# The first half of a state-space input product taken by pairs of token parts, between the parts of its norm

## The chip, the cores and the metric

One core of a Trainium2 chip runs the whole program. The time is the device time of one execution, in microseconds (us); it was 1764.43 us as the median of three runs.

## What is computed

Two transformer-like blocks over 512 tokens of 1024 channels, all in fp32. The change lies at the seam of the two: the layer norm at the end of the first block, then the root-mean-square norm and the input product of the second block's state-space mixer.

```python
x = _layernorm(DEEPNORM_ALPHA * x + ffn, ln2_g[l], ln2_b[l])      # end of the first block
...
h = rms_norm(x, mix_norm[layer])                                   # second block, layer 0
u = (h @ w_in).reshape(bsz, seq, SSM_GROUPS, SSM_GROUP)            # 64 groups of 16 channels
# then a scan along the tokens in each group, computed by chunks of T = 8 tokens (64 chunks)
```

## The kernel before

**Numbers.** Each fp32 operand of a large product is split into a high and a low part, and a product takes three matmuls (high-high, high-low, low-high). Activations lie turned, as `a_hi` and `a_lo` [channel in partition, 8 channel blocks, 512 tokens]. Weights pass through a ring of six slots in chunks of 512 KB: SP (SyncE) loads a chunk into `w_raw` when the slot's last chunk has been used (L1141), ScalarE (ACT) scales it by the norm's gain (L1190, two instructions, for these chunks alone) and makes the high part (L1195), GpSimd (POOL) makes the low part (L1045). The low part lies where the raw chunk lay, so a slot is free only when TensorE has used both. How far ACT makes chunks ahead is set by `make(count)`, held back by `limit`; a step that reads a PSUM bank first makes LEAD = 4 chunks ahead of that bank's.

**The seam.** The last down product of the first block's feed-forward runs tile by tile (four tiles of 128 tokens; `rows_by_tile`). Vector engine (DVE) work for a tile `t`: add the product to `x_rows` (L1693, which frees the bank), statistics (L1707, L1713), two passes of the layer norm (L1721, L1723). ACT then squares and sums the row (L1225), takes the root (L1226), and writes the normed row to `xh` (L1392, two buffers), with the root of the next tile's variance (L1369) between. TensorE turns each tile of `xh` by eight transposes into two banks (`mix0[0](t)`, L465), ACT copies them as high part into `a_hi` (L1204) and DVE makes the low part into `a_lo` (L1629). The token order in `a_hi` is changed on the way (`tile_split_s5`): column s*64 + c holds token s of chunk c, so that a matmul over 128 columns gives two token places of all 64 chunks.

**The product.** `w_in` is taken in two column halves. The first half ran as `rows_product`: four banks, one for each 128 columns; for each of four weight chunks all four banks get their 6 matmuls, so that a chunk is done with after 24 matmuls. The second half runs as `rows_by_tile` with the rounds of the state-space recurrence between its parts (`beside_rows`): the eight transposes of `s5_states` need all rows of the first half in `u_c` (they wait for bank ("u", 0, 3) to be freed). The rows go there by `even_rows` on DVE (L2117) and `odd_rows` on ACT (L1411), 64 partitions each.

In between lie other jobs. TensorE works on the recurrence's tables in batches of four groups (`prepare`); ACT evicts the last one, batch 15, in `s5_batch_out` (L1262, L1266), DVE finishes it in L2005, and SP stores it. After the last chunk of the first half ACT issues six loads of stored tables ("records" 0 and 1, L954, L959), SP issues records 2 and 3 behind the load of c7.

The chunks of the first half are called c0 to c3 here, those of the second c4 to c7.

## Time and profile before

| | |
|---|---|
| median of three runs | 1764.43 us (1764.03 to 1764.68) |
| the profiled execution, its own time | 1764.41 us |
| its span | 1762.4 us |
| mean granted TensorE clock | 0.991 of full |
| busy: TensorE matmul, DVE, ACT, GpSimd | 98%, 45%, 38%, 35% |
| idle before the third and fourth turn of the norm | 3.60 and 2.77 us |
| first and last matmul start of the first half product | 599.17, 623.47 us |

The times of the profile are counted from the start of the span; the 2 us between span and time lie around it. An engine's idle time is put down in brackets before an instruction with the work that released it. "PEclk" is the granted TensorE clock as a share of full speed (1.00 is 2.4 GHz, 0.50 is 1.2 GHz).

### The profile page before, as it was taken

The page shows a single profiled execution, that of the slowest core. Times are in us where ns is not written, and L with a number is a line of the kernel's source. Part 1 is how long each engine was busy: PE and PEld are TensorE (multiplying, and loading weights), DVE is VectorE, ACT ScalarE, POOL GpSimd, SP SyncE. Part 2 cuts the span into 40 slices and gives each one's busy share as a digit, 9 for nine tenths or more (in the row PEclk, how much of TensorE's full clock was granted, in tenths as well). Part 3 has the DMA queues.
Part 4 walks back from the last instruction along what each step waited for, and adds up shares of the span by engine and source line. Part 5 has one row for each costly group of instructions (what it writes and reads, how often), then busy time and mean ns, then how long its engine had stood idle before and what let it go on. Part 6 is the DMA issues. An engine that isn't in the chain of part 4 may idle for free.

```text
span 1762.4 us, 22364 instructions
## 1 busy us (share of the span) xinstructions
PE 1721.4 (98%) x8814; PEld 1417.5 (80%) x8814; DVE 793.2 (45%) x1454; ACT 676.2 (38%) x1184; POOL 624.0 (35%) x299
## 2 busy tenths in 40 slices
PE   8999999999999898999999999999899999999999
PEld 6887888887787687789888888888766888888887
DVE  3876899586766547333111111138774411111111
ACT  3333244243243756433222212276764332122221
POOL 5423203304204322424453534434711245345342
PEclk9999999999999899999999999999999999999999
DMA  9422245444445457223333233222201243332322
GB/s 244 96 74 83 72 125 155 148 133 131 140 125 172 142 194 245 80 67 114 97 95 96 93 100 102 84 76 70 73 1 37 72 115 98 94 99 86 107 90 78
DMA packets 241287, 189.58 MB, mean 108 GB/s; under 512 B 40481, under 2 KB 198305, under 8 KB 241185
## 3 DMA queue, kind: packets, MB, share of 16 engines
q1 hardware_dynamic: 239312, 182.79, 34.9%
q10 hardware_dynamic: 1872, 5.37, 0.9%
q8 instruction: 71, 1.16, 0.3%
q14 instruction: 32, 0.25, 0.0%
HBM read 168.73 MB, written 19.40 MB: 107 GB/s over the span
## 4 chain that ended last, share of the span: by engine, by line
PE 88%; DVE 6%; ACT 3%; issue 1%; DMA 1%; POOL 1%; DVEq 0%; SPq 0%; ACTq 0%
PE ps L383 14%; PE ps L385 14%; PE ps L384 14%; PE ps L409 10%; PE ps L411 10%; PE ps L410 10%; PE ps L440 3%; PE ps L442 3%; PE ps L441 3%; PE ps L867 1%; PE ps L897 1%; DVE x_rows L1723 1%; PE ps L859 1%; PE ps L877 1%; ACT w_hi L1195 1%
## 5 line engine op out<-in xcount | busy, mean ns | idle before, releaser
L1045 POOL TENSOR_TENSOR w_lo<-w_raw,w_hi 128x1024 fp32r<-128x1024 f32 (+4 forms) x251 | 587.4, 2350 | 1077.6 <-ACT w_hi L1195 1077.4
L383 PE MATMUL ps<-a_hi,w_hi 128*128 128x512 f32 (+1 forms) x1184 | 442.1, 373 | 0.0
L384 PE MATMUL ps<-a_lo,w_hi 128*128 128x512 f32 (+1 forms) x1184 | 440.4, 372 | 0.0
L385 PE MATMUL ps<-a_hi,w_lo 128*128 128x512 f32 (+1 forms) x1184 | 440.4, 372 | 0.0
L1195 ACT ACTIVATE w_hi<-w_raw 128x1024 fp32r<-128x1024 f32 (+3 forms) x283 | 283.1, 1019 | 207.9 <-DMA w_raw<-in_ffn_w_gate_up_dram 70.7
L383 PEld LDWEIGHTS ps<-a_hi,w_hi 128*128 128x128 f32 x1184 | 223.0, 188 | 40.1 <-issue 1.9
L385 PEld LDWEIGHTS ps<-a_hi,w_lo 128*128 128x128 f32 x1184 | 223.0, 188 | 38.8
L384 PEld LDWEIGHTS ps<-a_lo,w_hi 128*128 128x128 f32 x1184 | 223.1, 188 | 38.3
L2200 DVE TENSOR_TENSOR ev<-ps,xh 128x512 f32<-128x512 f32 x44 | 30.4, 692 | 411.9 <-PE ps L385 382.9
L409 PE MATMUL ps<-w_hi,h_hi 128*128 128x512 f32 x444 | 176.6, 398 | 2.7 <-DVE x_rows L1693 2.7
L411 PE MATMUL ps<-w_hi,h_lo 128*128 128x512 f32 x444 | 175.9, 396 | 0.0
L410 PE MATMUL ps<-w_lo,h_hi 128*128 128x512 f32 x444 | 175.7, 396 | 0.0
L1693 DVE TENSOR_TENSOR x_rows<-ps,x_rows 128x512 f32<-128x512 f32 x72 | 49.2, 690 | 219.5 <-PE ps L411 189.2
L1211 ACT ACTIVATE h_hi<-ev 128x512 fp32r<-128x512 f32 x66 | 41.8, 633 | 235.0 <-DVE ev L2200 195.5
L409 PE MATMUL ps<-w_hi,a_hi 128*128 128x512 f32 (+1 forms) x320 | 126.1, 394 | 1.8 <-DVE a_lo L1629 1.8
L410 PE MATMUL ps<-w_lo,a_hi 128*128 128x512 f32 (+1 forms) x320 | 124.7, 390 | 0.0
L411 PE MATMUL ps<-w_hi,a_lo 128*128 128x512 f32 (+1 forms) x320 | 124.5, 389 | 0.0
L409 PEld LDWEIGHTS ps<-w_hi,h_hi 128*128 128x128 f32 x444 | 84.0, 189 | 23.7 <-issue 4.4
L411 PEld LDWEIGHTS ps<-w_hi,h_lo 128*128 128x128 f32 x444 | 83.9, 189 | 19.8
L410 PEld LDWEIGHTS ps<-w_lo,h_hi 128*128 128x128 f32 x444 | 84.1, 189 | 19.5
L440 PE MATMUL ps<-w_hi,a_hi 128*128 128x512 f32 (+2 forms) x240 | 89.9, 375 | 5.5 <-POOL w_lo L1045 2.2
L1297 ACT ACTIVATE xh<-ps 128x512 f32<-128x512 f32 x44 | 26.3, 598 | 166.4 <-PE ps L385 166.4
(346 smaller groups left out, 2314.6 us busy)
## 6 DMA issues: line engine op xcount, KB each, us to landing
w_raw<-in_ffn_w_gate_up_dram SPq DMA_DIRECT2D x88, 512.0 KB, 3.8
w_raw<-in_w_up_dram SPq DMA_DIRECT2D x44, 512.0 KB, 4.0
w_raw<-in_ffn_w_down_dram SPq DMA_DIRECT2D x40, 512.0 KB, 3.8
w_raw<-in_w_in_dram SPq DMA_DIRECT2D x20, 512.0 KB, 4.3
w_raw<-in_w_down_dram SPq DMA_DIRECT2D x20, 512.0 KB, 3.9
s_records<-stage SPq DMA_DIRECT2D x16, 544.0 KB, 5.3
w_raw<-in_ssm_w_glu_dram SPq DMA_DIRECT2D x16, 512.0 KB, 3.9
rec<-s_records SPq DMA_DIRECT2D x14, 544.0 KB, 5.1
```

The source lines that it names most:

```text
L383: pe.matmul(bank, wh, xh_, start=first, stop=False)
L384: pe.matmul(bank, wh, xl_, start=False, stop=False)
L385: return pe.matmul(bank, wl, xh_, start=False, stop=last)
L409: pe.matmul(o, ah[:, k + kk, s], wh[:, kk, :], start=(n == 0 and kk == 0), stop=False)
L410: pe.matmul(o, ah[:, k + kk, s], wl[:, kk, :], start=False, stop=False)
L411: m = pe.matmul(o, al[:, k + kk, s], wh[:, kk, :], start=False, stop=end)
L440: pe.matmul(o, ah[:, k + kk, s], wh[:, kk, :], start=(k + kk == 0), stop=False)
L441: pe.matmul(o, ah[:, k + kk, s], wl[:, kk, :], start=False, stop=False)
L442: m = pe.matmul(o, al[:, k + kk, s], wh[:, kk, :], start=False, stop=end)
L1045: pool.tensor_tensor(w_lo[:, n % RING, 0:w], w_raw[:, n % RING, 0:w], w_hi[:, n % RING, 0:w].bitcast(F), ALU.subtract).then_inc(lo_made, 1)
L1195: act.activation(w_hi[:, n % RING, 0:w], w_raw[:, n % RING, 0:w], ACT.Copy).then_inc(hi_made, 1)
L1693: ins = v.tensor_tensor(o, b, o, ALU.add)
```

## The change

The first half no longer waits for all four turned tiles. A new token order puts the first 256 tokens at the even columns and the last 256 at the odd ones: column s*64 + 2c + q holds token s of chunk 32q + c. `rows_by_pair` multiplies the even columns (pair q = 0: two banks, four weight chunks, 48 matmuls) and then the odd ones (q = 1) with the same four chunks, which stay in the ring until the second pair has used them. Its first wait is for tiles 0 and 1. The turn of tile 2 stands behind its second chunk, that of tile 3 behind its fourth.

ACT and DVE follow. ACT makes c0 and c1 before batch 15's eviction, splits tiles 0 and 1 together, and makes c2 and c3 between the rows of tile 2 and the splits of tile 2. DVE splits tiles 0 and 1 together before it adds tile 3. A bank of the first half now holds four token places of 32 chunks, so `even_rows` and `odd_rows` take two instructions of 32 partitions each for each bank (four more on either engine). In the second half the rows come out with the two token halves interleaved; `s5_turned` puts them in order for batches 8 to 15 while it copies. The counts of chunks, of matmuls and of bytes are as before.

```diff
--- before.py
+++ after.py
@@ -418,6 +418,34 @@
                     if between:
                         between(n + 1)
 
+            def pair_columns(a, k, q, i):
+                return a[:, k, :].rearrange("p (c q) -> p q c", q=2)[:, q, i * P:i * P + P]
+
+            def rows_by_pair(stage, w, ah, al, nk, c0, cn, per, wait_q, gain, after):
+
+                parts = []
+                for q in range(2):
+                    banks = [open_bank((*stage, 2 * q + i)) for i in range(2)]
+                    pe.wait_ge(lo_ready, wait_q(q))
+                    for n, k in enumerate(range(0, nk, per)):
+                        if q == 0:
+                            parts.append(take_chunk(rows_of(w, k, per, c0, cn), per, cn, gains[:, gain, k:k + per]))
+                        wh, wl = parts[n]
+                        for i in range(2):
+                            o = banks[i][:, 0:cn]
+                            for kk in range(per):
+                                end = k + kk == nk - 1
+                                xh_, xl_ = (pair_columns(a, k + kk, q, i) for a in (ah, al))
+                                pe.matmul(o, xh_, wh[:, kk, :], start=(k + kk == 0), stop=False)
+                                pe.matmul(o, xh_, wl[:, kk, :], start=False, stop=False)
+                                m = pe.matmul(o, xl_, wh[:, kk, :], start=False, stop=end)
+                            if end:
+                                over = close_bank((*stage, 2 * q + i), m)
+                        if q and not end:
+                            chunk_over(m)
+                        after(q, n)
+                chunk_done.append(over)
+
             def rows_by_tile(stage, w, ah, al, nk, c0, cn, per, row0=0, wait_t=None, after=None, gain=None, late=False):
 
                 banks = [None if late else open_bank((*stage, t)) for t in range(TT)]
@@ -701,11 +729,14 @@
 
             ffn("f1", w_up[0], w_down[0], (FF, 0), ln1_turner, prepare, mix0_first)
 
-            for t in range(1, TT):
-                mix0[0](t)
-            mixed = n_split[0]
-            rows_product(("u", 0), ssm_w_in_2[0], a_hi, a_lo, KT, 0, HALF, 2, gain=2,
-                         wait_k=lambda k: mixed - (k < KT // 2))
+            def later_turns(q, n):
+                if (q, n) in ((0, 1), (0, 3)):
+                    mix0[0](2 + n // 2)
+
+            mix0[0](1)
+            chunks_at["u"] = len(chunk_done)
+            rows_by_pair(("u", 0), ssm_w_in_2[0], a_hi, a_lo, KT, 0, HALF, 2, lambda q: mix0[1](2 * q + 1), 2,
+                         later_turns)
             held = []
 
             def s5_bank(name, open_=open_bank):
@@ -967,9 +998,16 @@
 
         def tile_split_s5(k0, t):
 
-            c = slice(t * P // T, (t + 1) * P // T)
-            dst = [a[:, k0:k0 + 4, :].rearrange("p k (s c) -> p k s c", s=T)[:, :, :, c] for a in (a_hi, a_lo)]
+            c = slice((t % 2) * P // T, (t % 2 + 1) * P // T)
+            dst = [a[:, k0:k0 + 4, :].rearrange("p k (s c q) -> p k s c q", q=2, s=T)[:, :, :, c, t // 2]
+                   for a in (a_hi, a_lo)]
             return dst
+
+        def step_rows(bank, j, i):
+
+            q, r = j // 2, slice(NC // 2 * i, NC // 2 * i + NC // 2)
+            return (u_c[NC // 2 * q:NC // 2 * q + NC // 2, 0:32, 4 * (j % 2) + i, :],
+                    bank[r, :].rearrange("c (g k) -> c g k", k=GK))
 
         def ev_s5(e):
             return e.rearrange("p (k c s) -> p k s c", k=4, s=T)
@@ -1304,7 +1342,8 @@
                         for half in range(2):
                             if (g, half) in down_batch:
                                 if down_batch[g, half] == NB:
-                                    limit[0] = chunks_at[("u", 0, 0)] - 3
+                                    limit[0] = chunks_at["u"] + 2
+                                    make(limit[0])
                                 s5_batch_out(down_batch[g, half] - 1)
                             if (g, half) == (2, 0):
                                 load_second_norm()
@@ -1381,22 +1420,35 @@
 
 
             whole = lambda t: (ln_ready, t + 1)
-            ln_deviation(down, 1, 0)
-            limit[0] += 1
-            make(limit[0])
-            for t in range(TT):
-                deviation("mix0", down, whole, t)
-                if t + 1 < TT:
-                    ln_deviation(down, 1, t + 1)
+            def mix0_rows(t):
                 act.wait_ge(rms_made, t + 1)
                 act.activation(xh[:, t % 2, :], x_rows[:, t, :], ACT.Copy, scale=st[:, 8 + t:9 + t])\
                    .then_inc(xh_ready, 1)
-                if t and t < TT - 1:
-                    split_tile("mix0", t - 1, to_a_s5)
-            split_tile("mix0", TT - 2, to_a_s5)
-            split_tile("mix0", TT - 1, to_a_s5)
+
+            def next_chunk():
+                limit[0] += 1
+                make(limit[0])
+
+            ln_deviation(down, 1, 0)
+            deviation("mix0", down, whole, 0)
+            ln_deviation(down, 1, 1)
+            mix0_rows(0)
+            deviation("mix0", down, whole, 1)
+            ln_deviation(down, 1, 2)
+            mix0_rows(1)
+            split_tile("mix0", 0, to_a_s5)
+            split_tile("mix0", 1, to_a_s5)
+            deviation("mix0", down, whole, 2)
+            ln_deviation(down, 1, 3)
+            mix0_rows(2)
+            next_chunk()
+            next_chunk()
+            split_tile("mix0", 2, to_a_s5)
+            deviation("mix0", down, whole, 3)
+            mix0_rows(3)
+            split_tile("mix0", 3, to_a_s5)
             limit[0] = 10 ** 6
-            make(chunks_at[("u", 0, 0)] + 1)
+            make(chunks_at["u"] + 5)
             for i in range(2):
                 act.wait_ge(st_out[i], 16 * (NB // 2))
                 act.wait_ge(k_out[i], 16 * (NB // 2) * T)
@@ -1407,7 +1459,12 @@
                 load_out_part(act, b_)
             def odd_rows(half, j):
                 b = at(("u", half, j))
-                act.wait_ge(u_even, 4 * half + j + 1)
+                if not half:
+                    act.wait_ge(u_even, 2 * j + 2)
+                    step(act.activation(*step_rows(b, j, 1), ACT.Copy))
+                    release(("u", half, j), act.activation(*step_rows(b, j, 3), ACT.Copy))
+                    return
+                act.wait_ge(u_even, 2 * TT + j + 1)
                 release(("u", half, j), act.activation(u_c[:, 32 * half:32 * half + 32, 2 * j + 1, :],
                                                        b[NC:P, :].rearrange("c (g k) -> c g k", k=GK), ACT.Copy))
 
@@ -1417,7 +1474,11 @@
             def s5_turned(b_):
                 if b_ >= RECS:
                     act.wait_ge(*closed(("y", b_ - RECS)))
-                release(("ut", b_), act.activation(u_t[:, b_ % RECS, :], at(("ut", b_))[:, 0:GB * NC], ACT.Copy))
+                o, b = u_t[:, b_ % RECS, :], at(("ut", b_))[:, 0:GB * NC]
+                if b_ >= NB // 2:
+                    o = o.rearrange("p (g q c) -> p g q c", g=GB, q=2)
+                    b = b.rearrange("p (g c q) -> p g q c", g=GB, q=2)
+                release(("ut", b_), act.activation(o, b, ACT.Copy))
 
             def s5_gelu(b_):
                 y = at(("y", b_))[:, 0:2 * P].rearrange("c (g t k) -> c t g k", g=GB, t=T // 2)
@@ -2102,18 +2163,23 @@
             rms(1)
             ln_rows(2, 1, ln_ready)
             split_tile("mix0", 0, to_a_s5)
+            split_tile("mix0", 1, to_a_s5)
             add(3)
             ln_stats(3)
             rms(2)
             ln_rows(3, 1, ln_ready)
-            split_tile("mix0", 1, to_a_s5)
+            split_tile("mix0", 2, to_a_s5)
             rms(3)
-            split_tile("mix0", 2, to_a_s5)
             split_tile("mix0", 3, to_a_s5)
             go(v.memset(zc[:, :, :, 0:1], 0.0))
             go(v.memset(zs[:, :, 0:1], 0.0))
             settle()
             def even_rows(half, j):
+                if not half:
+                    b = full(v, ("u", half, j))
+                    v.tensor_copy(*step_rows(b, j, 0)).then_inc(u_even, 1)
+                    v.tensor_copy(*step_rows(b, j, 2)).then_inc(u_even, 1)
+                    return
                 v.tensor_copy(u_c[:, 32 * half:32 * half + 32, 2 * j, :],
                               full(v, ("u", half, j))[0:NC, :].rearrange("c (g k) -> c g k", k=GK))\
                  .then_inc(u_even, 1)
```

TensorE, behind the turn of tile 1 (`xh` to `ps`; 128x512 are product matmuls). Before, and then with the change:

```order
L465 MATMUL ps<-ident,xh 128x128 [waits bank_free0,xh_ready]
L465 MATMUL ps<-ident,xh 128x128 x3
L465 MATMUL ps<-ident,xh 128x128 [waits bank_free1]
L465 MATMUL ps<-ident,xh 128x128 x3
L465 MATMUL ps<-ident,xh 128x128 [waits bank_free2,xh_ready]
L465 MATMUL ps<-ident,xh 128x128 x3
L465 MATMUL ps<-ident,xh 128x128 [waits bank_free3]
L465 MATMUL ps<-ident,xh 128x128 x3
L465 MATMUL ps<-ident,xh 128x128 [waits bank_free4,xh_ready]
L465 MATMUL ps<-ident,xh 128x128 x3
L409 MATMUL ps<-w_hi,a_hi 128x512 [waits hi_made,lo_ready,lo_made]
L410 MATMUL ps<-w_lo,a_hi 128x512
```

```order
L493 MATMUL ps<-ident,xh 128x128 [waits bank_free0,xh_ready]
L493 MATMUL ps<-ident,xh 128x128 x3
L493 MATMUL ps<-ident,xh 128x128 [waits bank_free1]
L493 MATMUL ps<-ident,xh 128x128 x3
L439 MATMUL ps<-w_hi,a_hi 128x512 [waits hi_made,lo_ready,lo_made,bank_free3,bank_free2]
L440 MATMUL ps<-w_lo,a_hi 128x512
L441 MATMUL ps<-w_hi,a_lo 128x512
L439 MATMUL ps<-w_hi,a_hi 128x512
```

The turns of tiles 2 and 3 are gone from this place, and the first product matmul waits for two weight semaphores, the splits of two tiles, and banks 2 and 3; 24 matmuls later the turn of tile 2 follows.

ACT, at the end of the last down product (w_raw<-w_raw,gains and w_hi<-w_raw are chunk making; k_s<-ps is batch 15's eviction; st<-st the root of tile 0's variance). Before, and then with the change:

```order
L1195 ACTIVATE w_hi<-w_raw 128x512 [waits w_landed5]
L1262 ACTIVATE k_s<-ps 16x112 [waits bank_full5,k_out1,tables_ready]
L1262 ACTIVATE k_s<-ps 16x112 x3
L1266 ACTIVATE stage_99<-ps 128x512 [waits bank_full4,st_out1]
L1369 ACT_TABLE_LOAD
L1369 ACTIVATE st<-st,eps_c 128x1 [waits var_ready]
L1190 ACTIVATE w_raw<-w_raw,gains 128x512 [waits w_landed0]
L1190 ACTIVATE w_raw<-w_raw,gains 128x512
L1195 ACTIVATE w_hi<-w_raw 128x1024 [waits act_step]
```

```order
L1233 ACTIVATE w_hi<-w_raw 128x512 [waits w_landed5]
L1228 ACTIVATE w_raw<-w_raw,gains 128x512 [waits w_landed0]
L1228 ACTIVATE w_raw<-w_raw,gains 128x512
L1233 ACTIVATE w_hi<-w_raw 128x1024 [waits act_step]
L1228 ACTIVATE w_raw<-w_raw,gains 128x512 [waits w_landed1]
L1228 ACTIVATE w_raw<-w_raw,gains 128x512
L1233 ACTIVATE w_hi<-w_raw 128x1024 [waits act_step]
L1300 ACTIVATE k_s<-ps 16x112 [waits bank_full5,k_out1,tables_ready]
L1300 ACTIVATE k_s<-ps 16x112 x3
L1304 ACTIVATE stage_99<-ps 128x512 [waits bank_full4,st_out1]
L1408 ACT_TABLE_LOAD
```

One chunk stood behind the first root; two stand ahead of the batch's eviction now.

ACT, behind the record loads (u_c<-ps are the odd rows of the first half). Before, and then with the change:

```order
L959 DMA rec_109<-s_records 128x1088
L1190 ACTIVATE w_raw<-w_raw,gains 128x512 [waits w_landed4]
L1190 ACTIVATE w_raw<-w_raw,gains 128x512
L1195 ACTIVATE w_hi<-w_raw 128x1024 [waits act_step]
L1190 ACTIVATE w_raw<-w_raw,gains 128x512 [waits w_landed5]
L1190 ACTIVATE w_raw<-w_raw,gains 128x512
L1195 ACTIVATE w_hi<-w_raw 128x1024 [waits act_step]
L1190 ACTIVATE w_raw<-w_raw,gains 128x512 [waits w_landed0]
L1190 ACTIVATE w_raw<-w_raw,gains 128x512
L1195 ACTIVATE w_hi<-w_raw 128x1024 [waits act_step]
L1411 ACTIVATE u_c<-ps 64x32x16 [waits u_even,bank_full6]
L1411 ACTIVATE u_c<-ps 64x32x16 [waits u_even,bank_full7]
```

```order
L990 DMA rec_109<-s_records 128x1088
L1464 ACTIVATE u_c<-ps 32x32x16 [waits u_even,bank_full2]
L1465 ACTIVATE u_c<-ps 32x32x16 [waits act_step]
L1464 ACTIVATE u_c<-ps 32x32x16 [waits u_even,bank_full3]
L1465 ACTIVATE u_c<-ps 32x32x16 [waits act_step]
L1228 ACTIVATE w_raw<-w_raw,gains 128x512 [waits w_landed5]
L1228 ACTIVATE w_raw<-w_raw,gains 128x512
L1233 ACTIVATE w_hi<-w_raw 128x1024 [waits act_step]
L1228 ACTIVATE w_raw<-w_raw,gains 128x512 [waits w_landed0]
L1228 ACTIVATE w_raw<-w_raw,gains 128x512
L1233 ACTIVATE w_hi<-w_raw 128x1024 [waits act_step]
L1464 ACTIVATE u_c<-ps 32x32x16 [waits u_even,bank_full0]
```

Three chunks (c4, c5 and c6; the records stood behind c3) came ahead of the four odd-row copies. Now the records stand behind c4, and the copies of two banks ahead of c5, those of the other two behind c6.

## Rows read from the trace of the kernel before

**Rows 1.** The page, section 1: busy us, share, instructions.

```profile
PE 1721.4 (98%) x8814; PEld 1417.5 (80%) x8814; DVE 793.2 (45%) x1454; ACT 676.2 (38%) x1184; POOL 624.0 (35%) x299
```

**Rows 2.** Timeline of PE: start us, us, engine, line, operation [idle before <-releaser].

```profile
581.35 1.04 PE L465 MATMUL ps<-ident,xh 128*128 128x128 f32 x8
...
591.74 1.97 PE L465 MATMUL ps<-ident,xh 128*128 128x128 f32 x8 [3.60 <-ACT xh L1392]
596.49 1.97 PE L465 MATMUL ps<-ident,xh 128*128 128x128 f32 x8 [2.77 <-ACT xh L1392]
599.17 0.77 PE L409 MATMUL ps<-w_hi,a_hi 128*128 128x512 f32 x1 [0.72 <-DVE a_lo L1629]
...
606.02 0.39 PE L409 MATMUL ps<-w_hi,a_hi 128*128 128x512 f32 x1
...
623.70 0.39 PE L440 MATMUL ps<-w_hi,a_hi 128*128 128x512 f32 x1
```

**Rows 3.** Windows: length, busy of PE, PEld, DVE, ACT, POOL, PEclk, DMA, GB/s.

```profile
592.00:599.00 7.00, 3.68 (x16) 2.88 (x15) 4.83 (x8) 5.33 (x11) 0.00 (x0) 0.50 0.51 155
```

**Rows 4.** Timeline of PE at the chunk c7.

```profile
630.17 0.47 PE L440 MATMUL ps<-w_hi,a_hi 128*128 128x512 f32 x1 [0.19 <-POOL w_lo L1045]
```

**Rows 5.** Timeline of ACT at batch 15 and at the first norm rows.

```profile
571.01 1.05 ACT L1262 ACTIVATE k_s<-ps 16x112 f32<-16x112 f32 x4 [10.39 <-PE ps L664]
...
579.77 1.14 ACT L1392 ACTIVATE xh<-x_rows,st 128x1024 f32<-128x1024 f32 x1
```

**Rows 6.** SP's issue of c1, and its time from issue to landing.

```profile
565.92 0.37 SPq L1141 DMA_DIRECT2D w_raw<-in_ssm_w_in_dram  x1
...
w_raw<-in_ssm_w_in_dram SPq DMA_DIRECT2D x1, 512.0 KB, 5.3
```

**Rows 7.** Timeline of ACT during the half product.

```profile
600.34 1.06 ACT L1195 ACTIVATE w_hi<-w_raw 128x1024 fp32r<-128x1024 f32 x1
...
605.12 0.82 ACTq L954 DMA_DIRECT2D rec<-s_records  x2
...
607.93 1.34 ACT L1190 ACTIVATE w_raw<-w_raw,gains 128x512 f32<-128x512 f32 x2 [1.90 <-issue]
...
616.34 1.34 ACT L1190 ACTIVATE w_raw<-w_raw,gains 128x512 f32<-128x512 f32 x2 [3.67 <-DMA w_raw<-in_ssm_w_in_dram]
```

**Rows 8.** Timeline of DVE in the norm.

```profile
573.08 0.69 DVE L1693 TENSOR_TENSOR x_rows<-ps,x_rows 128x512 f32<-128x512 f32 x1
...
587.47 1.28 DVE L1629 TENSOR_TENSOR a_lo<-ps,a_hi 128x512 fp32r<-128x512 f32 x2
588.67 0.68 DVE L1693 TENSOR_TENSOR x_rows<-ps,x_rows 128x512 f32<-128x512 f32 x1
...
590.11 0.21 DVE L1713 BATCH_NORM_AGGREGATE st<-st 128x2 f32<-128x12 f32 x1
```

**Rows 9.** Timeline of POOL (GpSimd), three low parts.

```profile
601.47 7.09 POOL L1045 TENSOR_TENSOR w_lo<-w_raw,w_hi 128x1024 fp32r<-128x1024 f32 x3 [21.24 <-ACT w_hi L1195]
```

**Rows 10.** Timeline of PE at 1167, and the windows view around it.

```profile
1167.48 0.37 PE L440 MATMUL ps<-w_hi,a_hi 128*128 128x288 f32 x1 [1.99 <-POOL w_lo L1045]
...
1166.00:1174.00 8.00, 6.52 (x39) 6.55 (x40) 1.68 (x3) 3.77 (x7) 3.16 (x2) 0.79 0.01 2
```

**Rows 11.** SP's issue of c6, and its time from issue to landing.

```profile
607.57 0.37 SPq L1141 DMA_DIRECT2D w_raw<-in_ssm_w_in_dram  x1
...
w_raw<-in_ssm_w_in_dram SPq DMA_DIRECT2D x1, 512.0 KB, 8.8
```

**Rows 12.** Line L1411: durations min/median/max in ns, first and last start.

```profile
L1411 ACT ACTIVATE u_c<-ps x8: 593/596/597, 620.7 to 659.1; 64x512 f32<-64x512 f32 x8
```

**Rows 13.** Line L1204 from 640 and in the norm; page, section 5.

```profile
L1204 ACT ACTIVATE a_hi<-ps x8: 1097/1116/1216, 655.5 to 721.2; 128x512 fp32r<-128x512 f32 x8
...
L1204 ACT ACTIVATE a_hi<-ps x8: 572/584/597, 585.6 to 598.5; 128x512 fp32r<-128x512 f32 x8
...
L383 PEld LDWEIGHTS ps<-a_hi,w_hi 128*128 128x128 f32 x1184 | 223.0, 188 | 40.1 <-issue 1.9
```

## The prediction

> **What bounds the kernel now.** First the busy shares: TensorE is busy for 98% of the span [rows 1], so what the change can win is idle or slowly clocked TensorE time, and the question is where it is. TensorE's timeline at the change answers: three idle places lie side by side [rows 2]. The third turn of the norm waits 3.60 us for its rows, the fourth 2.77 us, and the first product of the state-space input waits 0.72 us more. The granted clock of that stretch is 0.50, the 1.2 GHz level [rows 3]; the matmuls run at that level until 604.4. From 599.17 to 606.02 lie 18 matmul starts in 6.85 us; the 78 starts from 606.02 to 623.70 take 17.68 us, 0.227 us each [rows 2], so the slow clock costs about 2.8 us of the product.
>
> I call the weight chunks of the two halves c0 to c3 and c4 to c7, and the matmul stream's arrival at c7 (630.17 before, where it waited 0.19 us for that chunk's low part [rows 4]) the end of the stage: behind it the code has the same work and TensorE is the bound again, so the gain or loss there is the gain or loss of the kernel.
>
> **Ideal saving.** The second turn is over at 588.1 (591.74 - 3.60). With two turns of 0.8 us (as 581.35 to 582.14 [rows 2]) and 96 matmuls of 0.227 us behind it and no wait, the half product would be over at 611.5 instead of 623.7. So at most 12.2 us are there. Both ACT and VectorE (DVE) get in the way, step by step:
>
> **1. Two chunks ahead of the last table batch.** ACT now makes c0 and c1 before it evicts the kernel block of batch 15, which it did at 571.01 [rows 5]. c1 is issued at 565.92 and lands 5.3 us later, at 571.2 [rows 6]. Making a chunk takes ACT 1.34 + 1.06 = 2.4 us [rows 7]. The eviction starts at 573.6, 2.6 us late. DVE's add of tile 0 began right behind it, at 573.08 [rows 8], and DVE then works without a real pause through the four tiles; so the whole norm shifts by 2.6 us. The first rows xh would be ready at 579.77 + 1.14 + 2.6 = 583.5 [rows 5], where TensorE wants them at 581.35 [rows 2]: 2.2 us of new idle, and the second turn ends at 590.3.
>
> **2. Start of the first pair.** DVE reaches its first splits at 587.47 + 2.6 = 590.1 and now makes four instead of two (1.28 us a pair [rows 8]): 592.7. The two banks of the pair are those of the down product's third and fourth tile, and the add of the fourth tile stands behind the four splits: 0.7 us more [rows 8]. So the pair starts at 593.4, after 3.1 us of idle. 24 matmuls at full clock take it to 598.9, the third turn to 599.7.
>
> **3. c2 and c3.** The statistics of tile 3 come 1.65 us after the start of its add (588.67 to 590.32 before [rows 8]), at 594.3; ACT then takes a root of 0.3 us and the rows of 1.14 us: 595.8. Then it makes c2 and c3, to 598.2 and 600.5. GpSimd adds 2.36 us for each low part (7.09 us for three [rows 9]): 600.5 and 602.9. TensorE at full clock would wait 0.8 us here. After the idle of 3.1 us I expect a stretch at 1.2 GHz: an idle of 1.99 us at 1167 was followed by one, and over the 8 us around it the mean granted clock was 0.79, so that 8 x 0.21 = 1.7 us of clock were lost [rows 10]. Of 1.7 us, 0.8 is hidden by this wait and 0.9 counts. Turn three ends at 601.4, c2 and c3 are used until 606.9, the fourth turn ends at 607.7.
>
> **4. Second pair.** It waits for the splits of tile 3: one ACT split 0.6 and one DVE split 0.7 behind the turn, 1.4 us with the gaps (0.72 before, where the slow turn hid the rest). 609.1, and 48 matmuls later 620.0. That is 3.7 us before the old 623.70.
>
> **5. The second half gives it back.** c0 and c1 are kept until the second pair has used them, so c6 can only be loaded into c0's slot at 609.1 + 2.7 = 611.8. ACT ends its last split at 608.4, makes c4 until 610.7 and begins to issue the state records 0.9 us before that, at 609.8. That is the distance of before: 605.12 against the end of c3 at 600.34 + 2 x 2.3 + 1.06 = 606.0 [rows 7]. So records and c6 still meet: 2.1 us after the first record, 2.45 before. I take the landing time of before, 8.8 us [rows 11]: c6 lands at 620.7. ACT finishes the record issues at 612.6 (2.8 us, to the 607.93 of before [rows 7]), makes four odd-row copies of tiles 0 and 1, and c5, until 617.5, and then waits for c6, until 623.1 with its making. Only then come the four odd-row copies of tiles 2 and 3, which have to be over before TensorE may turn the first states. A copy of 64 partitions takes 0.596 us [rows 12]. No row shows one of 32 partitions: between half and the same, I take the same, since the elements in a partition are the same: 2.5 us for four, 625.6. TensorE arrives at 622.7 and idles 2.9 us. ACT makes c7 from 625.6 to 628.0, and GpSimd its low part to 630.4. TensorE had c7 at 630.17 before, and now at 630.5.
>
> **Sum.** Idle and clock removed -3.7 us at the end of the half product, wait for the odd rows and c7 +4.0 (10.5 us from there to c7 against 6.5): +0.3. The profiled execution has 1764.41 us beside a span of 1762.4 and a median of 1764.43, so both bases agree; the forecast is **1764.7 us**.
>
> DVE's even-row copies double as well, at no cost: the four of tiles 0 and 1 fall into the second pair, and the four of tiles 2 and 3, 0.7 us each from 618.6 on, are over at 621.4, before ACT is ready for them at 623.1. Without that cover they would bound ACT; rival B counts that. SP issues the same transfers in the same order, with later slots. Batch 15's stores stand between c3 and c4; c4 is wanted at 608.4 by ACT, long after.
>
> **The step of 8 bytes.** The new column order makes ACT and DVE write the split rows, and TensorE load its stationary tiles, at every second fp32. No such row exists. The nearest is a split written with a step of 64 bytes: ACT 1.116 us against 0.584 for the one with contiguous runs [rows 13]. So the bounds are nothing and +0.53 us per split, and for a load of 0.188 us [rows 13] nothing and double. I take nothing and keep the other end for a rival. The Trainium skill's page "SBUF — State Buffer", section "Door 1: The DMA port swizzle", says that SBUF works in lines of 16 bytes and that two accesses to a line are enough for full bandwidth; two fp32 at 8 bytes fall into one line. By that rule the term is zero, and the 64-byte row agrees with it.
>
> **Rivals.** *A, slower:* the 8-byte step costs like the 64-byte one. Four DVE splits before the first pair give about +1.6, the last tile +0.9, in sum 1764.7 + 2.5 = 1767.2 for the writers alone. If the loads double as well, the matmul distance goes from 0.227 to 0.376 us: 96 x 0.15 = 14.3, less some 1.5 of waits: about 1780. It turns slower once a load costs over 0.227 us, the cover that the running matmul gives. For it: a 1.9-fold row. Against it: the 8 times larger step. *B, faster:* c6 does not meet the records and lands after 5.3 us, as c1 did. Then ACT has c6 by 619.9, the odd rows follow the closing of the banks (620.0, plus two copies on each engine) to 622.6, no state waits, and c7's low part is there at 627.4: -2.8, so 1761.6; without the slow stretch 0.9 less, 1760.7. For it: some of the records may be through when c6 is issued, if the first pair ends later than the records' issue assumes. Against it: both follow the same pair, and their distance (2.1 against 2.45 us) hardly changes. *C, the clock:* the idle of 1.4 us before the second pair is also followed by a slow stretch: +1.7 in the pair, about +1.3 at the end: 1766.0. For it: 0.72 us of idle among slow turns left the clock at 0.50 before. Against it: the pair ahead is full of matmuls.
>
> **Chances.** Forecast 0.51, C 0.10, B 0.29, A 0.10. A measurement can tell about 0.2%, 3.5 us. Forecast and C (0.61) lie within; of B about 0.22 lies beyond (it needs the full clock or an early norm as well), 0.07 within; of A 0.06 beyond; errors of several steps in one direction take 0.09 from what lies within and add 0.01 to faster and 0.08 to slower. Faster 0.23, same 0.63, slower 0.14. The range takes most of B and the mild part of A: 1760.0 to 1768.0; what it leaves out is about 0.17.
>
> **What would show it.** ACT's eviction of batch 15 near 573.6, and xh of tile 0 at 583.5. The first pair beginning near 593.4 behind DVE's add of tile 3. The half product ending near 620. A wait of some 3 us of the first states' turn for ACT's odd rows, ACT waiting for c6 before them. c7 reached near 630.5. Stationary loads at 188 ns and splits at 0.59 us. The forecast is wrong if c6 lands within 6 us of its issue, if ACT isn't held by c1's landing, or if the loads at the 8-byte step are longer.

## The result and the profile after

| | before | after |
|---|---|---|
| median of 20 runs, us | 1764.0 (1761.58 to 1765.0) | 1766.55 (1763.94 to 1768.69) |
| ratio to before | | 1.0017, 95% interval 1.0011 to 1.0023 |
| profiled execution, us, and its span | 1764.41, 1762.4 | 1763.94, 1761.9 |
| c7 reached | 630.17 [rows 4] | 629.58 |
| end of the half product | 623.70 [rows 2] | 619.57 |
| from c7 to the end of the span | 1132.2 | 1132.3 |

The change costs 2.6 us by the medians (0.14%; 0.17% by the ratio), just inside the 0.2% that I called no change; the interval reaches a little beyond. The profiled execution is the fastest of the 20 runs of the change, so its profile shows the stage, and it doesn't by itself show why the median is 2.6 us above it.

The page, section 1, answers [rows 1]: TensorE (PE) is busy 2 us less, with the same instructions.

```profile
PE 1719.4 (98%) x8814; PEld 1415.1 (80%) x8814; DVE 795.8 (45%) x1458; ACT 679.0 (39%) x1188; POOL 624.0 (35%) x299
```

Timeline of TensorE in the profile after, against [rows 2, 4]: two idle places of 3.60 and 2.77 us are gone, and there are new ones at the first turn (1.55), ahead of the first pair (2.84), at its third chunk c2 (0.46), ahead of the second pair (1.74) and of the first states' turn (2.16).

```profile
583.00 1.09 PE L493 MATMUL ps<-ident,xh 128*128 128x128 f32 x8 [1.55 <-ACT xh L1425]
...
592.69 0.48 PE L439 MATMUL ps<-w_hi,a_hi 128*128 128x512 f32 x1 [2.84 <-DVE x_rows L1754]
...
598.36 1.03 PE L493 MATMUL ps<-ident,xh 128*128 128x128 f32 x8
599.85 0.48 PE L439 MATMUL ps<-w_hi,a_hi 128*128 128x512 f32 x1 [0.46 <-POOL w_lo L1083]
...
605.52 1.04 PE L493 MATMUL ps<-ident,xh 128*128 128x128 f32 x8
608.30 0.48 PE L439 MATMUL ps<-w_hi,a_hi 128*128 128x512 f32 x1 [1.74 <-DVE a_lo L1690]
...
619.57 0.39 PE L468 MATMUL ps<-w_hi,a_hi 128*128 128x512 f32 x1
...
624.62 0.46 PE L756 MATMUL ps<-ident,u_c 64*128 64x64 f32 x4 [2.16 <-ACT u_c L1465]
625.00 0.67 PE L468 MATMUL ps<-w_hi,a_hi 128*128 128x512 f32 x1
...
629.58 0.47 PE L468 MATMUL ps<-w_hi,a_hi 128*128 128x512 f32 x1
```

The windows view of the same profile (length, busy of PE, PEld, DVE, ACT, POOL, PEclk, DMA, GB/s), against [rows 3]: the first pair runs at full clock here. The 0.83 of the second window is the stretch at the 1.2 GHz level that follows the states' idle: at 625.00 above a matmul takes 0.67 instead of 0.39 us.

```profile
592.00:599.00 7.00, 6.31 (x30) 5.34 (x31) 4.25 (x7) 5.34 (x8) 1.68 (x1) 1.00 0.66 203
620.00:630.00 10.00, 7.81 (x35) 5.68 (x34) 1.57 (x4) 7.58 (x12) 5.26 (x5) 0.83 0.80 317
630.00:638.00 8.00, 8.00 (x42) 6.47 (x41) 5.26 (x12) 3.48 (x8) 0.81 (x2) 1.00 0.21 68
```

ACT, against [rows 5, 7]: the eviction of batch 15 starts at 573.05 instead of 571.01, since c1 is only there at 570.60. The records are issued from 608.66, c6 is waited for until 619.66, the four odd-row copies of 32 partitions follow, then c7.

```profile
570.60 1.34 ACT L1228 ACTIVATE w_raw<-w_raw,gains 128x512 f32<-128x512 f32 x2 [1.26 <-DMA w_raw<-in_ssm_w_in_dram]
...
573.05 1.06 ACT L1300 ACTIVATE k_s<-ps 16x112 f32<-16x112 f32 x4
...
608.66 0.82 ACTq L985 DMA_DIRECT2D rec<-s_records  x2
...
619.66 1.34 ACT L1228 ACTIVATE w_raw<-w_raw,gains 128x512 f32<-128x512 f32 x2 [3.38 <-DMA w_raw<-in_ssm_w_in_dram]
...
622.12 0.59 ACT L1464 ACTIVATE u_c<-ps 32x512 f32<-32x512 f32 x1
```

DVE, against [rows 8]: the add of tile 0 (L1754) is 2.05 us late, and the add of tile 3 stands behind four low parts at 591.91.

```profile
575.13 0.69 DVE L1754 TENSOR_TENSOR x_rows<-ps,x_rows 128x512 f32<-128x512 f32 x1
...
589.51 2.48 DVE L1690 TENSOR_TENSOR a_lo<-ps,a_hi 128x512 fp32r<-128x512 f32 x4
591.91 0.68 DVE L1754 TENSOR_TENSOR x_rows<-ps,x_rows 128x512 f32<-128x512 f32 x1
```

SP's issue of c6 and its time from issue to landing, against [rows 11]:

```profile
611.36 0.37 SPq L1179 DMA_DIRECT2D w_raw<-in_ssm_w_in_dram  x1
...
w_raw<-in_ssm_w_in_dram SPq DMA_DIRECT2D x1, 512.0 KB, 8.3
```

The rows at the step of 8 bytes, against [rows 13]: durations of line L1242 (min/median/max in ns), the lines view of PE's weight loads with the mean in ns, and two rows of TensorE's timeline in the second pair. A split takes 0.610 us against 0.584, a load 193 ns against 188. From 610.00 to 615.60 lie 24 matmul starts, 0.233 us each, where the half product before had 0.227 at full clock [rows 2]: over the 96 matmuls that is 0.6 us.

```profile
L1242 ACT ACTIVATE a_hi<-ps x8: 592/610/648, 587.7 to 606.7; 128x512 fp32r<-128x512 f32 x8
...
L439 PEld LDWEIGHTS ps<-w_hi,a_hi 128*128 128x128 f32 x31 | 6.0, 193 | 6.8 <-issue 3.0 <-DVE a_lo L1690 1.9 <-ACT w_hi L1233 0.7
...
610.00 0.39 PE L440 MATMUL ps<-w_lo,a_hi 128*128 128x512 f32 x1
...
615.60 0.39 PE L440 MATMUL ps<-w_lo,a_hi 128*128 128x512 f32 x1
```

The second half, which loads contiguous columns, stands 0.227 us apart with loads of 188 ns in the same profile (from 619.57 on). That the longer load makes the longer distance is not shown, though: the down product before it stands 0.232 us apart with loads of 188 ns.

### The profile page after: what moved, and what is told of

It reads as the page before. It is cut to its first block, busy times and chain, and to the rows that moved or that the text cites. A ratio compares the mean times of both kernels' runs of the same rounds, so it can differ in the third digit from the quotient of the medians.

```text
span 1761.9 us, 22372 instructions
## 1 busy us (share of the span) xinstructions
PE 1719.4 (98%) x8814; PEld 1415.1 (80%) x8814; DVE 795.8 (45%) x1458; ACT 679.0 (39%) x1188; POOL 624.0 (35%) x299
## 4 chain that ended last, share of the span: by engine, by line
PE 87%; DVE 6%; ACT 3%; DMA 2%; issue 2%; POOL 1%; DVEq 0%; SPq 0%; ACTq 0%
PE ps L383 14%; PE ps L384 14%; PE ps L385 14%; PE ps L409 10%; PE ps L411 9%; PE ps L410 9%; PE ps L468 3%; PE ps L470 3%; PE ps L469 3%; PE ps L898 1%; PE ps L928 1%; DMA w_raw<-in_ssm_w_in_dram 1%; PE ps L890 1%; PE ps L908 1%; DVE x_rows L1784 1%
## 5 line engine op out<-in xcount | busy, mean ns | idle before, releaser
L1754 DVE TENSOR_TENSOR x_rows<-ps,x_rows 128x512 f32<-128x512 f32 x72 | 49.2, 690 | 219.5 <-PE ps L411 189.3
L409 PE MATMUL ps<-w_hi,a_hi 128*128 128x512 f32 (+1 forms) x288 | 112.3, 390 | 1.1 <-DVE a_lo L1690 1.1
L410 PE MATMUL ps<-w_lo,a_hi 128*128 128x512 f32 (+1 forms) x288 | 111.1, 386 | 0.0
L411 PE MATMUL ps<-w_hi,a_lo 128*128 128x512 f32 (+1 forms) x288 | 111.1, 386 | 0.0
```

Of the source, the lines that this page charges most:

```text
L409: pe.matmul(o, ah[:, k + kk, s], wh[:, kk, :], start=(n == 0 and kk == 0), stop=False)
L410: pe.matmul(o, ah[:, k + kk, s], wl[:, kk, :], start=False, stop=False)
L411: m = pe.matmul(o, al[:, k + kk, s], wh[:, kk, :], start=False, stop=end)
L1754: ins = v.tensor_tensor(o, b, o, ALU.add)
```

## The experiments

Each kernel was timed beside the kernel before on its chip; where no interval stands, the medians are compared. Unless said otherwise they compute all of the result.

### c1 later, records earlier, both

e1 gives ACT only c0 ahead of batch 15, c1 behind the root of tile 0:

```diff
-                                    limit[0] = chunks_at["u"] + 2
+                                    limit[0] = chunks_at["u"] + 1
...
             ln_deviation(down, 1, 0)
+            next_chunk()
             deviation("mix0", down, whole, 0)
```

> The change, but ACT makes only c0 ahead of batch 15's eviction and c1 behind the root of tile 0's variance. Theory 1 (the whole norm is shifted by c1's landing): the eviction falls back from 573.05 to about 571.0, DVE's add of tile 0 from 575.13 to 573.1, the idle of 1.55 us before the first turn goes, the first pair starts near 590.6 instead of 592.69, and c7 is reached 2 us earlier, near 627.6; the median falls by 2 to 3 us against the change. Rival (ACT's time in the norm is what counts, wherever c1 stands): the first pair starts where it did, and the time stays within 0.7 us of the change.

Measured: 1764.23 us (before on this chip 1763.71), ratio 1.0001, interval 0.9992 to 1.0010. TensorE's timeline in its profile: no wait at the first turn, the steps behind it 1.2 to 2.3 us earlier than in the change (590.44 for 592.69, 623.41 for 624.62), but the states' turn still waits 2.34 us, and c7 comes at 628.38, 1.2 us earlier and not 2. Here the first pair has the slow stretch that the profile of the change hasn't.

```profile
581.14 1.04 PE L493 MATMUL ps<-ident,xh 128*128 128x128 f32 x8
...
590.44 0.48 PE L439 MATMUL ps<-w_hi,a_hi 128*128 128x512 f32 x1 [2.50 <-DVE x_rows L1755]
...
623.41 0.46 PE L756 MATMUL ps<-ident,u_c 64*128 64x64 f32 x4 [2.34 <-ACT u_c L1466]
```

e2 moves the issues of records 0 and 1 on ACT from behind c4 to ahead of the last tile's splits:

```diff
             mix0_rows(3)
-            split_tile("mix0", 3, to_a_s5)
-            limit[0] = 10 ** 6
-            make(chunks_at["u"] + 5)
             for i in range(2):
...
                 load_out_part(act, b_)
+            split_tile("mix0", 3, to_a_s5)
+            limit[0] = 10 ** 6
+            make(chunks_at["u"] + 5)
```

> The change, but ACT issues the records behind the rows of tile 3 (near 603.3, where it idled 2.84 us) instead of behind c4. Theory 2 (c6 is late because it shares the DMA queues with the records, and the odd rows stand behind it): c6 lands within 6 us of its issue at 611.1 instead of 8.6, the wait of 2.16 us before the first states' turn falls below 0.5, c7 is reached near 626.5 instead of 629.58; the median falls by about 3 us. Rival (c6 is late because its slot is free so late): c6 still lands near 619, c7 moves by less than 1 us.

Measured: 1763.66, ratio 1.0001 (0.9992 to 1.0010). In its profile, the timeline of ACT (records, then c6), the landing time of c6, and the timeline of TensorE:

```profile
601.98 0.82 ACTq L985 DMA_DIRECT2D rec<-s_records  x2
...
614.57 1.34 ACT L1228 ACTIVATE w_raw<-w_raw,gains 128x512 f32<-128x512 f32 x2 [0.47 <-DMA w_raw<-in_ssm_w_in_dram]
```

```profile
w_raw<-in_ssm_w_in_dram SPq DMA_DIRECT2D x1, 512.0 KB, 3.8
```

```profile
621.97 0.46 PE L756 MATMUL ps<-ident,u_c 64*128 64x64 f32 x4
...
626.94 0.76 PE L468 MATMUL ps<-w_hi,a_hi 128*128 128x512 f32 x1 [0.98 <-POOL w_lo L1083]
```

c6 is issued at 610.77 and lands in 3.8 us instead of 8.3, ACT waits 0.47 us for it instead of 3.38, and the states' turn doesn't wait. c7 is reached 2.6 us earlier than in the change. The wait of that turn is thus a matter of where the records' transfers lie, and not of how late c6's slot is free. The matmul at 626.94 takes 0.76 us, though: a slow stretch begins there without the states' idle.

e3 does both edits.

> Both edits. If theories 1 and 2 both hold, the gains add: c7 near 624.5, the median 5 to 6 us under the change and so about 3 us under the kernel before. If the chain behind them is bound by the making of c2 and c3 or by the second pair's wait for tile 3, the sum is less than the parts.

Measured: 1760.27, ratio 0.9980 (0.9972 to 0.9989). Against the change's 1766.55, e1 is 2.3 us lower, e2 2.9, both 6.3: the gains add up, with 1.1 us over that nothing here explains (the change was timed beside another kernel before, 1764.0 against 1763.71). Timeline of TensorE: c7 at 624.79, 5.4 us ahead of before.

```profile
589.21 0.76 PE L439 MATMUL ps<-w_hi,a_hi 128*128 128x512 f32 x1 [2.52 <-DVE x_rows L1755]
...
624.79 0.47 PE L468 MATMUL ps<-w_hi,a_hi 128*128 128x512 f32 x1 [0.98 <-POOL w_lo L1083]
```

### Is it the clock?

e5 is the change once more.

> The change as it is, once more, on the chip of the next three runs. Theory 1 to 3 and rivals alike: 1 to 3 us above the kernel before, c7 reached between 629.5 and 632.5 us, by the number of stretches at 1.2 GHz.

Measured: 1765.81 (before 1763.57), ratio 1.0010 (1.0001 to 1.0019). Its profiled execution took 1766.08, near the median. Timeline of TensorE, then the windows view:

```profile
599.55 1.03 PE L493 MATMUL ps<-ident,xh 128*128 128x128 f32 x8
...
625.28 0.46 PE L756 MATMUL ps<-ident,u_c 64*128 64x64 f32 x4 [2.29 <-ACT u_c L1465]
...
630.25 0.47 PE L468 MATMUL ps<-w_hi,a_hi 128*128 128x512 f32 x1 [0.98 <-POOL w_lo L1083]
...
631.31 0.63 PE L469 MATMUL ps<-w_lo,a_hi 128*128 128x512 f32 x1
```

```profile
592.00:599.00 7.00, 6.67 (x22) 5.43 (x23) 3.89 (x7) 5.70 (x8) 2.04 (x1) 0.76 0.61 194
630.00:638.00 8.00, 7.75 (x33) 6.17 (x34) 3.10 (x7) 2.40 (x6) 1.47 (x5) 0.79 0.22 68
```

The first pair has its slow stretch (0.76), so the third turn comes 1.19 us later than in the profile above; and a second stretch lies behind c7 (0.79 in its window, 1.00 above), where each matmul from 631.31 takes 0.63 us. Eight intervals of 0.43 us instead of 0.23 lie there: 1.6 us, and from c7 to the end of the span it is 1133.85 us instead of 1132.3. The same code had one slow stretch in this stage in one execution and two in another, at different places.

What a stretch costs hangs on its place. From the states' turn to c7 it is 4.96 us in the profile above, with the stretch (624.62 to 629.58), and 4.97 us here, without it (625.28 to 630.25): without the stretch TensorE waits 0.98 us for c7's low part, so the stretch is free there. Behind c7 no wait covers it, and it costs its 1.6 us.

In the change's 20 runs the mean time falls with the mean granted clock: 1764.6 us at 0.994 (2 runs), 1765.8 at 0.993 (5), 1767.3 at 0.992 (8), 1767.7 at 0.991 (5). The mean clock is a rough gauge only: both profiled executions have 0.994 and lie 2.1 us apart. e5's one has two stretches in the stage, but none from 690 to 740, where the other has one (clock 1.00 against 0.97) that costs it nothing: e5 is 2.3 us behind at either end of that window.

e4 and e6 put transposes of the identity into banks about to be written, at the idle places of the change, so that TensorE isn't idle there. Nothing reads them. In e4 they stood behind the wait for the pair's banks, 24, 14 and 20 ahead of the two pairs and of the states. e6 puts them ahead of that wait: 12 before the first turn, 26 and 16 before the pairs, 18 before the states. The edit shown is e6's:

```diff
+            def idle_turns(count, ahead=0):
+                i = len(freed) + ahead
+                pe.wait_ge(*freed[i - 8])
+                for n in range(count):
+                    pe.transpose(ps[:, i % 8, (n % 4) * P:(n % 4) * P + P], ident[:, :], ident[:, :])
...
+                    if q == 0:
+                        idle_turns(26, 2)
                     banks = [open_bank((*stage, 2 * q + i)) for i in range(2)]
```

> The change, with transposes of the identity matrix that nothing reads in the three idle places of TensorE: 24 before the first pair, 14 before the second, 20 before the first states' turn. Theory 3 (the median of 20 runs lies 2.6 us above the profiled execution because in most executions a stretch at 1.2 GHz follows one of these idle places): no row of the stage is at 0.50, and the median falls by 2 us or more, with a spread under 2 us. Rival (the spread has another cause, as DMA landings): the median stays within 0.7 us of the change and the spread at 4 us.

Measured: 1769.14, ratio 1.0032 (1.0020 to 1.0044), a miss: by TensorE's timeline the turns began only where the idle ended, and delayed the stage by their own 4.47 us. It tells nothing of the clock.

```profile
593.81 4.47 PE L423 MATMUL ps<-ident 128*128 128x128 f32 x24 [2.29 <-issue]
```

> The change with transposes of the identity that nothing reads, now ahead of each wait: 12 before the first turn, 26 before the first pair's banks are waited for (in e4 the 24 stood behind that wait, so they ran after it and cost 4.5 us themselves), 16 before the second pair, 18 before the first states' turn. Theory 3 (idle places of TensorE are followed by stretches at 1.2 GHz in most executions, and these make the median 2.6 us longer than the profiled execution): the mean granted clock of every run is 0.994 or more, the median lies 2 us or more under the change. Rival: the clock is as before and the median within 0.7 us.

Measured: 1763.74, ratio 1.0001 (0.9992 to 1.0009), 2.1 us under e5 on the same chip. TensorE's timeline shows 26 turns in the idle place ahead of the pair and 0.61 us of idle left at the states; c7 comes at 630.35, no earlier than in e5.

```profile
590.02 3.00 PE L425 MATMUL ps<-ident 128*128 128x128 f32 x26
...
630.35 0.47 PE L479 MATMUL ps<-w_hi,a_hi 128*128 128x512 f32 x1 [0.98 <-POOL w_lo L1096]
```

So the arrival at c7 is unmoved and the median is still 2.1 us lower, with a mean clock of 0.9952 against e5's 0.9929 over the runs: 0.0023 x 1762 = 4 us of clock, of which half shows in the time. The two profiled executions (1764.63 and 1766.08) say where: from c7 to the end of the span it is 1132.25 us in e6, at full clock from 630 to 638, and 1133.85 in e5. The intervals of the medians overlap, so this supports the clock's part and isn't proof of its size.

e7 is e3 with 22 and 16 such turns ahead of the pairs; e8 is the kernel before with 32 ahead of the third and of the fourth turn.

> Both edits of e3, with 22 such transposes before the first pair and 16 before the second. Theory 3: the median falls by another 1 to 1.5 us under e3, to about 1759, and its spread narrows to 2 us. Rival: no difference to e3.

Measured: 1761.31, ratio 0.9984 (0.9975 to 0.9993); mean clock 0.9945 against e3's 0.9942. The expected gain over e3 isn't there. In its profile the first pair has no slow stretch (e3 has one) and c7 comes at 624.32, 0.5 us ahead of e3's, no more: the pair takes 1.4 us longer in e3 (589.21 to 596.30, against 5.7 us), but e7 waits 0.47 us for c2's low part behind it, which e3 does not, and its pair starts 0.3 us later.

> The kernel before the change, with 32 such transposes ahead of the third and 32 ahead of the fourth turn. Theory 3 (2.8 us of the old half product were lost to the 1.2 GHz stretch behind its idle places): the 13 slow matmuls from 599.17 run at full clock, the half product ends 2 to 3 us earlier, and the median falls by 2 to 2.8 us, so that the change's saving at that place is partly a saving of clock. Rival: the transposes stand in the way of the turns, and the time stays or rises.

Measured: 1761.89, ratio 0.9986 (0.9977 to 0.9994), 1.7 us under before. TensorE's timeline:

```profile
587.08 3.66 PE L425 MATMUL ps<-ident 128*128 128x128 f32 x32
...
598.16 0.47 PE L409 MATMUL ps<-w_hi,a_hi 128*128 128x512 f32 x1 [1.48 <-DVE a_lo L1637]
...
626.52 0.47 PE L446 MATMUL ps<-w_hi,a_hi 128*128 128x512 f32 x1 [0.19 <-POOL w_lo L1053]
```

The product starts at 598.16 at full speed and c7 comes at 626.52, 3.65 us earlier. The profiled execution took 1759.21 us, 5.2 less than the profiled one of the kernel before, so its early arrival is kept in full. The other 1.6 us come from another slow stretch: the idle of 1.99 us that [rows 10] shows with a stretch behind it (0.79 over 8 us) stands at 1163.61 here, as long, and the clock stays full. The next wait behind it tells the price: it is reached at 1276.63 in the kernel before and at 1271.17 here, 109.15 us behind that idle against 107.56. The windows view of e8, and TensorE's timeline in the kernel before and in e8:

```profile
1162.00:1170.00 8.00, 6.39 (x50) 6.42 (x51) 3.06 (x7) 3.90 (x7) 3.25 (x2) 1.00 0.01 2
```

```profile
1276.63 0.66 PE L885 MATMUL ps<-ident,inv_b 128*128 128x128 f32 x4 [1.77 <-DVE inv_b L2327]
```

```profile
1271.17 0.66 PE L893 MATMUL ps<-ident,inv_b 128*128 128x128 f32 x4 [1.77 <-DVE inv_b L2335]
```

The median is higher since the runs fall in two groups: three of 11 at 1759.0 to 1759.6 us with a mean clock of 0.997, as in the profile, and eight at 1761.0 to 1762.4 with 0.995. Arrival and time don't part here; the profile and the median are different executions.

e8's interval overlaps those of e3 and of e12 below (0.9978). So it isn't shown that the reordering with both edits gains more than filling the idle places of the old order does.

### The same edits in the kernel before

e9 moves the records ahead of c1 to c3 in the kernel before, where they stood behind c3:

```diff
-            limit[0] = 10 ** 6
-            make(chunks_at[("u", 0, 0)] + 1)
             for i in range(2):
...
                 load_out_part(act, b_)
+            limit[0] = 10 ** 6
+            make(chunks_at[("u", 0, 0)] + 1)
```

> The kernel before, with ACT issuing the records of the next block ahead of making chunks c1 to c3 instead of behind c4. My theory: c6 then lands within some 6 us of its issue instead of 8.8, but TensorE waited only 0.19 us for c7 in the kernel before, so that earlier landing is covered: time within 0.7 us of the kernel before. Rival 1: the gain of e2 (some 3 us) was not that of the wait for the states, but of the records' place itself, and shows here too: 1761. Rival 2: the making of c1 to c3, some 2.8 us later, delays the second turn: slower by up to 2.8 us.

Measured: 1762.91 (before 1763.65), ratio 0.9998 (0.9989 to 1.0006). Landing of c6 and TensorE's timeline:

```profile
w_raw<-in_ssm_w_in_dram SPq DMA_DIRECT2D x1, 512.0 KB, 4.3
```

```profile
598.34 0.77 PE L409 MATMUL ps<-w_hi,a_hi 128*128 128x512 f32 x1 [0.72 <-DVE a_lo L1629]
...
629.05 0.47 PE L440 MATMUL ps<-w_hi,a_hi 128*128 128x512 f32 x1 [0.18 <-POOL w_lo L1045]
```

c6 lands in 4.3 instead of 8.8 us and nothing is gained by it: c7 is 1.1 us earlier, 0.8 of which the product was ahead already at its start (598.34 against 599.17). The late landing was covered there; the change took the cover away.

e10 makes c0 and c1 ahead of batch 15 in the kernel before:

```diff
-                                    limit[0] = chunks_at[("u", 0, 0)] - 3
+                                    limit[0] = chunks_at[("u", 0, 0)] - 1
+                                    make(limit[0])
...
-            limit[0] += 1
-            make(limit[0])
```

> The kernel before with c0 and c1 made ahead of batch 15 and nothing else of the change. My theory: the norm starts 2.0 us later (as in the profile of the change), the first turn waits about 1.5 us, every later step of the stage is as much later, c7 at about 632; 1.5 to 2 us slower than the kernel before. Rival: the time ACT spends ahead of batch 15 is saved behind it, so the later splits start as before: within 0.5 us of the kernel before, c7 at 630.2.

Measured: 1764.52, ratio 1.0005 (0.9996 to 1.0013). The stage does as expected, by TensorE's timeline: the first turn waits (2.15 us, expected 1.5), the product starts 3.0 us late, c7 comes 1.9 us late. The last row is of the windows view.

```profile
583.98 1.09 PE L465 MATMUL ps<-ident,xh 128*128 128x128 f32 x8 [2.15 <-ACT xh L1391]
...
602.19 0.77 PE L409 MATMUL ps<-w_hi,a_hi 128*128 128x512 f32 x1 [0.72 <-DVE a_lo L1628]
...
632.08 0.47 PE L440 MATMUL ps<-w_hi,a_hi 128*128 128x512 f32 x1 [0.18 <-POOL w_lo L1045]
...
1168.00:1176.00 8.00, 6.85 (x53) 6.88 (x54) 3.46 (x8) 3.90 (x9) 2.85 (x2) 1.00 0.01 2
```

The median shows only 0.9 us of the 1.9, and the interval holds both theories. The profiled execution, 1764.52 us against 1764.41, shows where its 1.9 us went: as in e8, the idle at 1169.15 (1.98 us) has no slow stretch behind it, and TensorE is 1.7 us late there and 0.1 us late at the next wait (1276.73 against 1276.63). The delay of the stage is real, and what hides it is a slow stretch that this execution lacks further on.

### A last wait, and the best version again

e11 is e3 with `pass_bank()` twice ahead of the first pair, so that its banks aren't those that DVE's add of tile 3 frees.

> e3_both with the first pair of products in the two banks that the eviction of tile 3's residual doesn't hold (the bank counter is moved on by two ahead of it). My theory: the pair's idle of 2.52 us is in its last part the wait for that bank; without it the pair starts some 0.7 us earlier, idle about 1.8 us, c7 at about 624.1 instead of 624.8, 0.7 us below e3 (up to 1.5 if the slow stretch goes with it). Rival: the split of tile 1 or the low part of c2 ends as late as the bank does, nothing moves: time of e3, 1760.3.

> e3_both once more, as the measure for e11 on the same chip and to see whether its lead over the kernel before comes again. My theory: ratio to the kernel before about 0.998 (1760 to 1761 us), since it has the pairs' 16 matmuls per loaded weight, no wait for c6 and no wait ahead of the first turn. Rival: the lead was that chip's or the clock's: ratio 1.000.

Measured: e11 1761.0, ratio 0.9983 (0.9974 to 0.9992); e12 1759.8, ratio 0.9978 (0.9968 to 0.9988). e12 confirms e3: 3.9 us under before, after 3.4 in e3. (Its expectation speaks of 16 matmuls per loaded weight; the page counts 8814 matmuls and 8814 loads in e12 as in the kernel before, so that is no reason.) e11 gains nothing over it. From second to third turn it takes 10.26 us against 10.70, so the bank's wait was worth 0.44 us there, too little to see in the time; and its profile has a slow stretch behind c7, where e12's has none.

## Why the prediction was right, and where its steps were off

No change (within 0.2%) and the range (1760.0 to 1768.0) held; the median lies 1.85 us over the forecast of 1764.7. The path is the one that was forecast, step by step. Some of the hit is luck: most steps came 0.4 to 0.9 us earlier than forecast, and that took off a part of what the clock added behind them.

- **Step 1, batch 15.** Shown: c1 holds the eviction. The shift was 2.04 us instead of 2.6, since c1 was there at 570.60 and not at 571.2; so the first turn's idle was 1.55 instead of 2.2. e1 takes it away, e10 brings it into the kernel before.
- **Step 2, the pair's start.** Behind the add of tile 3, as forecast: 592.7 against 593.4, idle 2.84 against 3.1.
- **Step 3, c2 and c3.** TensorE waited 0.46 us for c2's low part (forecast 0.8). The slow stretch came in e5 and e1 and not in the profiled execution, where the fourth turn was at 605.52. With it, in e5, it was at 606.01 (forecast 606.9). e5's pair started 0.36 us earlier than the profiled one and was 0.49 us later at the fourth turn, so the stretch cost 0.85 us there, of the 0.9 that the forecast took.
- **Step 4, second pair.** Started 608.30 (forecast 609.1) after 1.74 us (1.4), over at 619.57 (620.0): 11.3 us for the 48 matmuls and not 10.9, at 0.233 us each.
- **Step 5, given back.** c6 was issued at 611.36, 2.7 us behind the first record, and landed in 8.3 us (forecast 611.8, 2.1 and 8.8; the forecast's own terms, 611.8 - 609.8, give 2.0); the odd rows cost 0.59 us each; the states' turn idled 2.16 us (forecast 2.9) and c7 came at 629.58, in e5 at 630.25 (forecast 630.5). e2 shows the mechanism: without the meeting of records and c6 this idle is 0. e9 shows why before didn't suffer from the same landing.
- **The sum.** The term that was mis-sized is the clock. I priced one slow stretch, in the first pair, at 0.9 us. The profiled execution has one in the stage, at the states, where it costs nothing, and with c7 0.6 us early it took 1763.94. e5, near the median, has two, in the first pair and behind c7; the second costs 1.6 us behind c7. With c7 at 630.25 and this 1.6 us the forecast's own sum gives 1766.1, and e5's profiled execution took 1766.08. That most of the 20 runs look like e5 is inferred from their lower mean clock; only one of the 20 has a profile, the fastest. e1 has two as well. That e6, which fills the idle places, comes to 1763.74 fits. The second stretch isn't tied to the states' idle alone: e2 and e11 have it at c7 without that idle, behind a wait of 0.98 us, where e3 and e12 have the same wait and none. Nor does the row that the price was taken from hold every time: the idle of 1.99 us at 1167 [rows 10] has a stretch behind it in the kernel before and none in e8 and e10. What decides it between executions stays open.
- **The step of 8 bytes.** The term was put at nothing and is small: 0.03 us for an ACT split, nothing for one of DVE, 5 ns for a load; but the matmuls of the pairs stand 0.233 us apart instead of 0.227, 0.6 us in sum. The rule of lines of 16 bytes, from the Trainium skill's page "SBUF — State Buffer", section "Door 1: The DMA port swizzle", gives zero; the splits agree with it to 0.03 us, and the load of 193 ns against 188 lies a little above it. The row that the prediction calls a step of 64 bytes has one of 32: it writes every eighth fp32 (`turned_back`, T = 8). It still has one fp32 in each line of 16 bytes, so the argument holds, but rival A's larger step was 4 times and not 8 times as large.
- **Rivals.** A fell: the step came nowhere near the price of that row (1.116 us against 0.584). B's condition (c6 not beside the records) did not arise by itself, but e2 made it: -2.9 us (2.15 below e5), where B said -3.1. C had the right kind of cost at the wrong place: the second pair ran at full clock after 1.74 us of idle.

## What to carry over

A reordering that keeps buffers longer moves the start of every load into them; ask what else is on the DMA queues at the new time, and what work stood in front of the late arrival before. Here the ideal of 12 us of idle and slow clock came to 3.4 to 3.9 us, and only once the two engines' small jobs (one chunk ahead of an eviction, six DMA issues) had been moved as well. And price the clock behind each idle place that the forecast creates, not only behind those that the old profile shows, and ask whether a wait stands behind it that hides a slow stretch. Before a profile is set against a median, look where its own execution lies among the runs.

## What was unexpected

- An instruction on 32 partitions takes as long as one on 64: 0.59 us on ACT (0.596 before [rows 12]), 0.68 us on DVE. Halving partitions to interleave two tiles doubled the count and the time.
- 512 KB of weights took 8.3 us beside ACT's record transfers and 3.8 us (e2) or 4.3 us (e9) once those had been issued some 7 us earlier (597.82 instead of 605.12 in e9).
- The same kernel had its slow stretches at different places in two executions, and a stretch can begin 0.8 us after TensorE has resumed (e5, 631.02 behind the start at 630.25).
- Behind the same idle of 1.98 to 1.99 us, some 540 us after the change, one execution has a slow stretch and another has none, and that moves the time by 1.6 us: as much as many of the differences that these runs were made to see.
